# Split rooms for the gate loads, a new order at x's first chunks and in the merges, and filler matmuls, in a one-core hybrid decoder block

## What is computed

```python
h = rmsnorm(x, norm1_g)                       # x: 256 x 1024
u, q, k, v, g_pool, g_attn = split(h @ w_in)  # 512 each, the two gates 1024
pool = pool_mixer(u) @ w_pool_up              # causal means over 2, 4, 8, 16
attn = stick_breaking_attention(rmsnorm(q), rmsnorm(k), v) @ w_attn_up
merged = sigmoid(g_pool) * pool + sigmoid(g_attn) * attn
x = x + merged @ w_out
h2 = rmsnorm(x, norm2_g)
# 32 experts, each token goes to its top 4
gu = h2[tokens of e] @ w_gate_up[e] + b_gate_up[e]         # 1024 -> 2048
y  = swiglu(gu) @ w_down[e] + b_down[e]                    # 1024 -> 1024
x  = x + sum over the chosen experts of gate * y
```

## Time and profile before

| | |
|---|---|
| median of 3 runs | 1100.51 us |
| the profiled execution | 1101.37 us |
| its span, first to last instruction | 1099.4 us |
| busy: TensorE matmul, weight load | 92%, 44% of the span |
| busy: VectorE, ScalarE, GpSimd | 24%, 17%, 2% |
| DMA moved | 431.09 MB, 62,072 packets, 32,824 of them of 8 KB or more |
| chain that ended last | TensorE 55%, DMA 36%, VectorE 4% |

### The profile page before, as it was taken

How to read it: one execution, slowest core, us unless ns; L and a number is a source line. 1 busy time by engine, 2 the same in 40 slices (tenths; PEclk the granted TensorE clock), 3 DMA queues, 4 the chain that set the end, 5 groups by cost and what they waited for, 6 DMA issues and landing times.

```text
span 1099.4 us, 14027 instructions
## 1 busy us (share of the span) xinstructions
PE 1011.1 (92%) x5712; PEld 484.3 (44%) x5712; DVE 266.9 (24%) x476; ACT 181.9 (17%) x253; POOL 18.1 (2%) x37
## 2 busy tenths in 40 slices
PE   7999998999999998999989898888888988898897
PEld 7989997333333333333333333333333333333332
DVE  6656685211111111111111111111111001111111
ACT  6377455110000000000000000000000000000001
POOL 3100001000000000000000000000000000000000
PEclk9999998999999999999999999999999999999999
DMA  9934669999999999999999999999999999999997
GB/s 329 329 124 130 230 242 383 429 423 424 426 427 428 426 427 423 424 426 426 427 427 429 426 425 427 426 426 426 426 426 425 425 427 427 426 429 427 424 426 284
DMA packets 62072, 431.09 MB, mean 392 GB/s; under 512 B 6412, under 2 KB 25376, under 8 KB 29248
## 3 DMA queue, kind: packets, MB, share of 16 engines
q1 hardware_dynamic: 62000, 430.74, 95.0%
q10 hardware_dynamic: 48, 0.01, 0.0%
HBM read 429.69 MB, written 1.05 MB: 392 GB/s over the span
## 4 chain that ended last, share of the span: by engine, by line
PE 55%; DMA 36%; DVE 4%; SPq 3%; issue 2%; ACT 1%; DVEq 0%
PE bank L1142 53%; DMA gate_ring<-in_w_gate_up_dram 31%; DMA down_ring<-in_w_down_dram 4%; SPq L356 2%; DVE area_x L1070 1%; PE bank L1484 1%; DVE area_m L732 1%; DMA raw<-in_w_in_dram 1%; DVE w_lo L732 0%; SPq L420 0%; DVE area_x L1054 0%; DVE area_x L732 0%; SPq L430 0%; DVE area_x L1055 0%; PE bank L1473 0%
## 5 line engine op out<-in xcount | busy, mean ns | idle before, releaser
L1142 PE MATMUL bank<-gate_ring,area_m 128*64 128x512 f32 x2048 | 460.5, 598 | 43.9 <-DMA gate_ring<-in_w_gate_up_dram 43.9
L1142 PEld LDWEIGHTS bank<-gate_ring,area_m 128*64 128x64 f32 x2048 | 146.0, 137 | 335.6 <-issue 260.7
L1142 PE MATMUL bank<-down_ring,area_x 128*64 128x512 f32 x1008 | 225.3, 596 | 17.2 <-DVE area_x L1070 12.2
L1054 DVE TENSOR_SCALAR area_x<-bank 128x512 f32<-128x512 f32 x28 | 19.4, 692 | 640.8 <-PE bank L1142 640.8
L1142 PEld LDWEIGHTS bank<-down_ring,area_x 128*64 128x64 f32 x1008 | 69.9, 137 | 153.7 <-issue 130.2
L1142 PE MATMUL bank<-area_m 128*128 128x128 bf16 (+5 forms) x976 | 116.4, 282 | 1.8 <-DVE area_m L732 1.1
L1142 PEld LDWEIGHTS bank<-area_m 128*128 128x128 bf16 (+4 forms) x976 | 73.7, 115 | 54.3 <-issue 49.9
L672 ACT ACTIVATE area_x<-area_x 128x512 f32<-128x512 f32 x28 | 17.6, 630 | 435.6 <-DVE area_x L1054 435.6
L680 ACT ACTIVATE area_m<-bank 64x512 f32<-64x512 f32 x56 | 33.1, 591 | 265.1 <-PE bank L1142 264.8
L1142 PE MATMUL bank<-w_hi,act_in 128*128 128x256 f32 x320 | 60.8, 289 | 2.2 <-DVE act_in L761 1.2
L1142 PE MATMUL bank<-act_in,w_hi 128*128 128x256 f32 x320 | 58.3, 284 | 0.0
(11 more groups left out here) (197 smaller groups left out, 480.8 us busy)
## 6 DMA issues: line engine op xcount, KB each, us to landing
gate_ring<-in_w_gate_up_dram SPq DMA_DIRECT2D x128, 2048.0 KB, 27.2
down_ring<-in_w_down_dram SPq DMA_DIRECT2D x126, 1024.0 KB, 21.3
raw<-in_w_in_dram SPq DMA_DIRECT2D x14, 1024.0 KB, 11.9
raw<-in_w_out_dram SPq DMA_DIRECT2D x4, 1024.0 KB, 5.9
raw<-in_w_pool_up_dram SPq DMA_DIRECT2D x2, 1024.0 KB, 11.6
raw<-in_w_attn_up_dram SPq DMA_DIRECT2D x2, 1024.0 KB, 5.1
early_down<-in_w_down_dram SPq DMA_DIRECT2D x2, 1024.0 KB, 9.8
raw<-in_w_in_dram SPq DMA_DIRECT2D x3, 512.0 KB, 7.5
```

The source lines that it names most:

```text
L1054: nc.vector.tensor_scalar(glu, glu_b[:], LIMIT, None, ALU.min).then_inc(s_glu, 1)
L1142: return nc.tensor.matmul(o, lhsT, rhs, start=start, stop=True, skip_group_check=True)
```

## The change

- **Rooms.** SLOT gives each gate load two rooms by their order of use, most of them apart. A load's semaphore belongs to its half and number, no longer to a room. The destination is a view of two pieces, `gate_ring[:, a:b + 1:b - a, :]`, and the source is written as two pieces of 8 KB per partition.
- **Waits of the first eight gate loads.** They follow the new rooms, half a block at a time.
- **x's first chunks.** Chunk 0 goes to bank 5 by itself, with its own count of s_xT; for the first two pieces ScalarE and VectorE take the activations ahead of the weights; the squares of x move from pieces 1 and 2 to pieces 3 and 4, the mean behind the loop.
- **The merges.** VectorE makes a unit's rest one unit later (`merged_rest`).
- **Fillers.** `run_idle` issues 128x128 float32 matmuls of the identity with itself: 6 ahead of x's transposes, 3 behind them, 5 behind the router, 3 ahead of the gather.

```diff
-        s_gl = [sem(f"gate_loaded{i}") for i in range(NSLOT // 2)]
+        s_gl = [[sem(f"gate_loaded{half}_{c}") for c in range(NGATE)] for half in range(2)]
...
+        def xT_of(k):
+            return bank[5][:, 0:S] if k == 0 else bank[k // 2][:, (k % 2) * S:(k % 2 + 1) * S]
...
-        SLOT = ((4, 5, 6, 7, 8, 9, 10, 11), (0, 1, 12, 13, 2, 3, 14, 15))
+        SLOT = ((4, 10, 5, 6, 7, 8, 9, 11), (0, 12, 1, 13, 2, 14, 3, 15))
...
             def gate_to(half, c):
-                s = SLOT[half][2 * c]
-                return gate_ring[:, s:s + 2, :].rearrange("p j n -> p (j n)"), s_gl[s // 2]
+                a, b = SLOT[half][2 * c:2 * c + 2]
+                return gate_ring[:, a:b + 1:b - a, :], s_gl[half][c]
...
-                sp.dma_start(dst, w_gate_up[0, e, 2 * c * P:2 * (c + 1) * P, :].rearrange("(p j) n -> p (j n)", j=2)) \
+                sp.dma_start(dst, w_gate_up[0, e, 2 * c * P:2 * (c + 1) * P, :].rearrange("(p j) n -> p j n", j=2)) \
...
-                             .rearrange("a (p j) n -> p (a j n)", j=2)).then_inc(done, 16)
+                             .rearrange("a (p j) n -> p (a j) n", j=2)).then_inc(done, 16)
...
             for c in range(NGATE):
-                if c < 3:
-                    sp.wait_ge(*used(7 + c, 1))
+                sp.wait_ge(*used((7, 8, 9, 9)[c], c // 3))
                 load_gate(0, 0, c)
             for c in range(NGATE):
-                if c % 2 == 0:
-                    sp.wait_ge(*used(10 + c // 2, 1))
+                sp.wait_ge(*used(10 + c // 2, c % 2))
                 load_gate(1, 1, c)
...
             for n in range(1 + KD // 2):
-                split(0, slice(n, n + 1))
-                for k in ((0,), (1,), (2, 3), (4, 5), (6, 7))[n]:
+                if n >= 2:
+                    split(0, slice(n, n + 1))
+                for k in range(KD)[FIRST_CHUNKS[n]]:
                     if k == 0:
                         act.wait_ge(s_cols, 1)
-                    if k % 2 == 0:
-                        act.wait_ge(s_xT, k // 2 + 1)
-                    nc.scalar.activation(act_in[:, 0, k, :], bank[k // 2][:, (k % 2) * S:(k % 2 + 1) * S], ACT.Copy,
+                    if k < 2 or k % 2 == 0:
+                        act.wait_ge(s_xT, k + 1 if k < 2 else k // 2 + 2)
+                    nc.scalar.activation(act_in[:, 0, k, :], xT_of(k), ACT.Copy,
                                          scale=cols[:, ROW_G1 + k:ROW_G1 + k + 1]).then_inc(s_hTh, 1)
-                if 1 <= n <= T:
-                    t = n - 1
+                if n < 2:
+                    split(0, slice(n, n + 1))
+                if n >= 3:
+                    t = n - 3
...
-                    dve.wait_ge(s_hTh, k // 2 * 2 + 2)
+                    dve.wait_ge(s_hTh, k + 1 if k < 2 else k // 2 * 2 + 2)
...
-                if n == 1 + T:
-                    dve.wait_ge(s_sumsq, T)
-                    mean(0, (tiny[:, 2:4], tiny[:, 0:2]), D)
+                if n < 2:
+                    split(0, slice(n, n + 1))
+            dve.wait_ge(s_sumsq, T)
+            mean(0, (tiny[:, 2:4], tiny[:, 0:2]), D)
...
+            def merged_rest(j):
+                dve.wait_ge(s_mhi, j + 1)
+                dve.wait_ge(s_mf, j + 1)
+                tt(act_in[:, 1, 2 * j:2 * j + 2, :], gate_p[:, 2 * j:2 * j + 2, :],
+                   carve(act_f[:, 0, :], 2 * j * S, 2, S), ALU.subtract).then_inc(s_mrg, 1)
...
                     tt(m, m, v, ALU.add).then_inc(s_mf, 1)
-                    dve.wait_ge(s_mhi, j + 1)
-                    dve.wait_ge(s_mf, j + 1)
-                    tt(act_in[:, 1, 2 * j:2 * j + 2, :], m, carve(act_f[:, 0, :], 2 * j * S, 2, S), ALU.subtract) \
-                        .then_inc(s_mrg, 1)
+                    if j:
+                        merged_rest(j - 1)
+                    if j == 3:
+                        merged_rest(3)
...
+            def run_idle(to, count):
+
+                for _ in range(count):
+                    mm(to[:, 0:P], ident[:], ident[:], True)
+
             pe.wait_ge(s_const, 1)
+            run_idle(bank[7], 6)
             for t in range(T):
...
+            run_idle(bank[7], 3)
...
             router(1, range(KD))
+            run_idle(t_b, 5)
...
+            run_idle(t_b, 3)
             pe.wait_ge(s_onehot, 1)
...
-                        pe.wait_ge(s_gl[s // 2], 16 * i + 16)
+                        pe.wait_ge(s_gl[half][k // 2], 16 * i + 16)
```

More of the change, by code:

```diff
@@ L757, in _ @@
             for n in range(1 + KD // 2):
-                split(0, slice(n, n + 1))
-                for k in ((0,), (1,), (2, 3), (4, 5), (6, 7))[n]:
-                    dve.wait_ge(s_hTh, k // 2 * 2 + 2)
-                    nc.vector.scalar_tensor_tensor(out=act_in[:, 1, k, :],
-                                                   in0=bank[k // 2][:, (k % 2) * S:(k % 2 + 1) * S],
+                if n >= 2:
+                    split(0, slice(n, n + 1))
+                for k in range(KD)[FIRST_CHUNKS[n]]:
+                    dve.wait_ge(s_hTh, k + 1 if k < 2 else k // 2 * 2 + 2)
+                    nc.vector.scalar_tensor_tensor(out=act_in[:, 1, k, :], in0=xT_of(k),
                                                    scalar=cols[:, ROW_G1 + k:ROW_G1 + k + 1],
@@ L1148, in _ @@
                 for k in range(KD):
-                    last = nc.tensor.transpose(bank[k // 2][:, (k % 2) * S + t * P:(k % 2) * S + (t + 1) * P],
-                                               x_sb[:, t, k * P:(k + 1) * P], ident[:])
-                    if t == T - 1 and k % 2:
+                    last = nc.tensor.transpose(xT_of(k)[:, t * P:(t + 1) * P], x_sb[:, t, k * P:(k + 1) * P], ident[:])
+                    if t == T - 1 and (k == 0 or k % 2):
                         last.then_inc(s_xT, 1)
```

## The result

| | before | after |
|---|---|---|
| median of 12 runs each, us | 1100.88 | 1105.08 (1103.09 to 1106.18) |
| ratio | | 1.0037, 95% interval 1.0030 to 1.0044 |
| span of the profiled run, us | 1099.4 | 1102.7 |
| profiled execution itself, us | 1101.37 | 1106.18 |

The changed kernel is slower by 0.37%, 3.3 to 4.8 us by the interval; the forecast was 2.9 us. The median of 1105.08 us is 1.7 us above the forecast of 1103.4 and outside the forecast's own range (1102 to 1104.5), inside the wide one (1097 to 1107). The spans of the two profiled executions differ by 3.3 us. They are single executions: the twelve of the change have spans of 1101.1 to 1103.6 us, median 1102.75, and the median span of the kernel before was 1098.9 to 1099.2 us in the sessions of the experiments, some 3.7 us less.

What follows compares the result with a forecast made beforehand. The DMA stream of expert weights was taken as the bound from near 250 us. Earlier stream -4.7, 8 KB runs +7.3, last loads +0.3 gave +2.9 us on the 1100.51 median: 1103.4 us, own range 1102 to 1104.5, wide range 1097 to 1107.

Steps and rivals of the forecast that it cites:

- rival A: Gate loads: all eight of a pair pay for 8 KB runs, 9.8 us instead of 7.3; 1106.0 us, chance 0.20.
- The price of 8 KB runs: Late gate loads, expert 4 on: 10.9 ns per extra run, 0.087 us a load, 7.3 us for 84 loads.
- Rival B: DMA queue from 250 us: 8 KB runs are free, only the gain is left; 1095.8 us, chance 0.24.
- Six of eight: Gate loads of a pair: two have adjoining rooms and stay one run, six pay; 12,288 more packets.
- The tail: Last four gate loads, needed as they land: 0.3 us more.
- The head: Start through the projection: x's chunk 0 first and fillers start block 1 at 22.1 against 23.5; 1.3 us gained.
- ScalarE: k0 7.0: Head: ScalarE takes x's chunk 0 at 7.0, ahead of the weights, so TensorE starts at 8.7, 1.0 us sooner.
- rival C: TensorE's path: fillers and order gain nothing, the stream gains 1.9 alone; block 1 at 23.5, 1106.5 us, chance 0.06.
- The merges: TensorE at 154 to 157 us: deferred rests remove both idles; 1.2 us gained.
- The gather: Router to gather, 183 to 187 us: eight fillers might hold the clock; 0.6 us taken of 0 to 1.5.
- The early loads: First eight gate loads: fewer rooms to wait for lets the DMA stream gain 1.9 us beyond TensorE's path.
- TensorE's 1.7 us of waiting there goes: TensorE at its down loads: its 1.7 us wait vanishes, so it is 4.8 us earlier and keeps up.

Runs made afterwards that it cites:

- experiment 1: Kernel before with only the split rooms (two 8 KB runs per partition), old waits and no other part of the change: 1109.93 us, ratio 1.0085.
- experiment 5: Kernel before with each gate load issued as two 1 MB loads of 8 KB runs, same bytes: 1111.34 us, ratio 1.0094.
- experiment 8: Changed kernel plus an early one-column ScalarE activation, so its table load runs ahead of the first waits: 1104.87 us, ratio 1.0030.
- experiment 9: Kernel before with only the merged rests made one unit later (merged_rest): 1099.25 us, ratio 0.9988.
- experiment 10: Changed kernel with old adjoining rooms and old waits, keeping order, merges and fillers, plus the early table load: 1098.81 us, ratio 0.9984.
- experiment 12: experiment 10 with the first sixteen rooms filled by sixteen 1 MB loads, each as its room comes free; later loads in adjoining rooms: 1097.07 us, ratio 0.9968.
- experiment 2: Changed kernel with the old adjoining rooms and old waits, keeping order, merges and fillers: 1099.42 us, ratio 0.9989.
- experiment 3: Changed kernel, split rooms kept, with the first eight gate loads waiting as before: 1107.87 us, ratio 1.0067.
- experiment 11: experiment 10 with experts 0 and 1 in split rooms with early waits, adjoining rooms from expert 2 on: 1101.69 us, ratio 1.0006.
- experiment 4: Kernel before with the split rooms and early waits, without the new order and fillers: 1106.09 us, ratio 1.0053.
- experiment 6: Kernel before with each gate load as two 1 MB loads by column half, 4 KB runs: 1138.2 us (two runs), ratio 1.0339.

## Why the prediction was right

The sign and the mechanism came out as forecast: the form of the loads costs more than the early start brings. The size is in part luck. Two terms were too large, the price by 1.3 us (7.3 for 6.0) and the gain by 2.0 (4.7 for 2.7), and these errors cancelled in part. By the medians the change costs 4.2 us and not 2.9. That is 0.9 us from rival A's 1106.0 and 1.7 from the forecast; it is the packets that shut A out, not the time.

- **The price of 8 KB runs.** Forecast 10.9 ns a run, 0.087 us a load, 7.3 us for 84 loads, pairs of 59.6. Measured 9.0 ns (9.3 with 4 KB runs), 0.072 us, 6.0 us, pairs of 59.48. The mis-sized term took its price from the gap between two rates of short stretches, 428.5 and 421 GB/s; the 1 KB row's 9.3 ns, which I had as a check, was the nearer of the two. The split rooms also cost some 2 us before the late loads (experiment 1, and the early loads below), where I had counted 0.3. Rival B (free) needed under 3 ns; the pair time shut it out, and experiment 5 its reason: 1 MB loads add nothing to the run's price. The Trainium skill ("DMA: Bandwidth & Descriptors", Why small descriptors are slow) gives a packet a fixed overhead of about three cycles, by which I estimated 2.4 us for the 84 loads (the time for it was 1098.2, not 1098.3); the runs show 6.0, so the measurement decides, and the page's figure is too small here.
- **Six of eight.** 12,288 more packets, and six loads' price in the pair time against eight loads' in experiment 5. As forecast.
- **The tail.** Forecast 0.3. From 593.87 to the end of the span the change takes 508.8 us, before 505.7: 3.1 us more, of which seven pairs at 0.43 explain 3.0. So 0.1.
- **The head.** Forecast 1.3; block 1 gains 0.84. The step that failed is "ScalarE: k0 7.0": the table load of 1.28 us stood in front of it (8.05). With it moved, block 1 gains 1.5 in one trace (experiment 8). The diagonal, the clause that limits the gain, was forecast ready at 21.3; it starts at 21.27 and is written by 21.75. Without fillers the gain is below zero (23.93): rival C's mechanism was right about the order and wrong about the fillers. These are differences of single executions. Over all traces, the matmul of rstd starts at 22.5 us on average in the six with the old head, at 21.6 in the three with the change's and at 21.3 in the four that load the table early, so the gains are near 0.9 and 1.2 us.
- **The merges.** No idle of TensorE at 154 to 157 us: the chain after runs through them, 120.37 us of TensorE from 48.49 on. Forecast 1.2; experiment 9 gives 1.1 of span, 1.9 by the medians.
- **The gather.** Forecast 0.6 of 0 to 1.5. Granted 0.89 instead of 0.50 in 183 to 187 us, and without fillers 0.69. The fillers do not settle this clock as they do the head's. From 176 to 188 us the mean granted clock is 0.72 to 0.79 in the seven traces without them; in the seven with them it is 1.00 in experiments 10 and 12, 0.86 in the change, 2 and 3, and 0.72 in 8 and 11. How much of the 1.7 us between with and without fillers is the gather's, and how much the head's 1.26, was not separated; the remainder is 0.4.
- **The early loads.** Their worth was about right: forecast 1.9, measured 2.0 by the spans, more by the medians (experiment 3). What failed is the step "TensorE's 1.7 us of waiting there goes". After: TensorE's waits from 232 to 250 us, three windows, and SyncE's issue of expert 3's first gate load:

```profile
PE bank L1153 <- DMA down_ring<-in_w_down_dram: 1.8, 2, 1.2
```

```profile
188.00:196.00 8.00, 8.00 (x42) 2.62 (x40) 0.40 (x3) 1.87 (x2) 0.00 (x0) 1.00 0.97 372
208.00:216.00 8.00, 8.00 (x39) 2.77 (x37) 1.20 (x3) 0.38 (x1) 0.00 (x0) 1.00 0.96 384
240.00:252.00 12.00, 12.00 (x58) 4.09 (x60) 0.00 (x0) 1.18 (x2) 0.00 (x0) 1.00 0.99 384
```

```profile
210.13 4.50 SPq L354 DMA_DIRECT2D gate_ring<-in_w_gate_up_dram  x2
```

  I had counted a dry spot as idle of the engines and nothing more. In these stretches, in which SyncE waits for TensorE to free rooms, the rate falls too, to 372 to 384 GB/s at a share of 0.96 to 0.99. So the stream's lead shrinks, and TensorE's wait at the down loads stays as it was (1.7 before). Expert 3's first load is issued at 210.13, 2.76 us sooner; expert 4's at 245.93, where the kernel before issues it at 248.59, 2.66 us sooner. Past 250 us the gain is thus near 2.7 us, not 4.7. TensorE starts expert 0 at 185.91, 2.7 us sooner than before (188.63; forecast 3.1), so it keeps its own gain up to there and the early loads add nothing to it. They save it, though. In experiment 3, with the split rooms and the old waits, TensorE starts expert 0 at 185.98, as early, but issues of expert 4 begin at 248.06, only 0.5 us sooner than before: 2.1 us are lost on the way, with a wait of 2.7 us at the down loads. In experiment 2, with adjoining rooms and the old waits, the lead goes only from 1.65 us (186.98) to 1.4 (247.22). So the split rooms cost nearly 2 us before 250 us, and the early waits bring 2.1. The forecast's 4.7 was 3.1 + 1.9 - 0.3. Its 0.3 for slower gate loads is the term that was mis-sized most, then the 3.1; the 1.9 was right. These are single executions, good to some tenths.

The sum redone with the measured terms: -2.7 + 6.0 + 0.1 = +3.4, and the spans of the two profiled executions differ by 3.3. The forecast's -4.7 + 7.3 + 0.3 was +2.9. By the medians the change costs 4.2 us and the rooms alone 8.8 (1109.93, against 1101.18 for the kernel before in the same session). Why the rooms alone cost more than the late loads' 6.0 is told in experiment 1 to within some 0.7 us. What stays open is what lies around the span.

## What to carry to other kernels

Where a stream of DMA sets the time, count its packets: here each extra run costs each engine 9 ns in loads of 1 and of 2 MB. Between 16 KB and 8 KB that is 1.5% of a gate load's time (0.072 of 4.9 us), while more loads with the same runs cost nothing. A layout that lets a few first loads start sooner must not be paid by every load behind them; give the first ones a form of their own, and watch that none of the later waits gets longer by it (experiments 11 and 12). When ScalarE's first activation is changed, look where its table load goes. And set a profiled execution beside the other executions of its kernel before taking its span apart: here experiment 1's was 1.9 us under the median.

## What the hardware showed that I had not expected

- **The table load moves with the first activation.** It takes 1.28 us. It stood at 3.43 before, ahead of that activation's wait for its weights (7.25), so it was hidden; at 6.76 after, behind the waits for the gains' columns and for x, so it was on the path; and at 3.44 with an early activation of one column. Why it runs ahead of the one wait and behind the others no run here shows.
- **The head's clock differs from run to run, and the fillers settle it.** Experiments 1 and 5 have the head's code of before, word for word. The timeline's matmul of rstd on the diagonal, with the rooms alone, then with two 1 MB loads:

```profile
21.33 0.60 PE L1142 MATMUL bank<-down_ring,area_m 128*128 128x256 f32 x2
```

```profile
23.99 0.60 PE L1147 MATMUL bank<-down_ring,area_m 128*128 128x256 f32 x2
```

  In the six profiles whose head is that of before it starts from 21.0 to 24.0; in the seven with fillers, from 20.99 to 21.91. The Trainium skill ("TensorE: Matmul & The Clock Gate", Part 1) says that the throttled state is the default and that activity releases it at a moment that varies; the traces agree. Of the 3 us, 2.3 are the projection's own time (12.46 us in experiments 1 and 4, 14.73 in experiment 5); the rest goes with the start, which follows the landing of weights and x. The fillers themselves ran at the low clock: six in 2.93 us, 0.49 each, where the five behind the router, at a granted clock of 1.00, take 1.36 us; the engine had only x to wait for.
- **The wait at the down loads came with a drop of the clock in some runs and without in others.** Where its longest piece was 2.6 to 5.5 us (experiments 1, 3, 6, 10, 11), a granted clock of 0.50 to 0.86 followed from 240 to 244 us; where it was 1.6 us or less (all others), it stayed at 1.00.
- **The stream slows before its engines show as idle:** 372 to 384 GB/s at a share of 0.96 to 0.99 where the issues are behind, against 423 past 250 us with the same runs. That the queue is nearly empty there is my reading; no view shows its length. And far into the stream SyncE is held in its issue: one of a late pair takes 6.51 us in the change, without loss there. With 4 KB runs the stream itself is slower in such stretches (experiment 6).
